# One Conformer mixer of an 11-stage transformer kernel: which channel tile VectorE convolves, in which order, and a norm worked out by halves of the tokens

## The chip, the cores and the metric

The kernel runs on one core of one Trainium2 chip. The metric is the device time of one execution in microseconds (us); lower is better. The core has a matrix engine (TensorE, PE in the rows; its weight loads are PEld), a vector engine (VectorE, DVE), a scalar engine (ScalarE, ACT), GpSimd (POOL) and SyncE (SP). SyncE issues most of the transfers, ScalarE some. Each engine works through its own instructions in order, and semaphores hold an instruction back until what it needs is there.

## The reference

A sequence of 256 tokens by 1024 channels, fp32, passes two attention layers and then four blocks, each a mixer and a squared-ReLU MLP. Block 0 and 3 have a retention mixer, block 2 a short convolution, block 1 the Conformer convolution, which runs once and is all that the change touches, but for one load:

```
def conformer_conv_mixer(x, w_pw1, b_pw1, w_dw, b_dw, ln_g, ln_b, w_pw2, b_pw2):
    h = x @ w_pw1 + b_pw1                      # 256 x 1024 by 1024 x 2048
    a, gate = jnp.split(h, 2, axis=-1)
    h = a * jax.nn.sigmoid(gate)
    h = causal_depthwise_conv(h, w_dw) + b_dw  # 31 taps along the tokens, each channel by itself
    hf = h.astype(F32)
    mean = jnp.mean(hf, axis=-1, keepdims=True)
    var = jnp.mean(jnp.square(hf - mean), axis=-1, keepdims=True)
    hf = (hf - mean) * lax.rsqrt(var + LN_EPS) * ln_g + ln_b
    h = jax.nn.silu(hf)
    return h @ w_pw2 + b_pw2                   # 256 x 1024 by 1024 x 1024
```

## The kernel before

All weights stream through the core once, in chunks of 512 rows by 512 columns (1 MB). Each chunk goes through three buffers: `raw` (loaded by SyncE), `wh` (its high part, a ScalarE cast, `high_to(c)` casts all chunks up to c), and `wl` (the rest, a VectorE subtraction, `low_to(c)`). TensorE multiplies high by high, high by low and low by high, so a product of a chunk takes 48 matmuls. There are three buffers of each kind, so `raw` of chunk c+3 is loaded when `wl` of chunk c is done, and `wh` of c+3 is cast when TensorE has used chunk c. The order of every engine is written out by hand; nothing is scheduled automatically.

The Conformer mixer has chunks +0 to +11 (counted from its first, `first["s", 1]`). Channels lie in 8 tiles of 128 partitions, the 256 tokens along the free dimension.

- Chunks +0 to +3 give gate and value of channel tiles 0 to 3, chunks +4 to +7 those of tiles 4 to 7. ScalarE takes the sigmoids, and `gated(b)` on VectorE makes the gated values `hp` of four tiles, in `HP`.
- Seven tiles are convolved by TensorE, one by VectorE. `four_taps` copies groups of tiles (`a`, `b`, `c` in `TAPS`) between partitions, so that 32 channels at four shifts fill 128 rows; each copy is 16 DMAs. `tap_squares(n)` on VectorE lays out the filter of the n-th tile in `CONV` as small diagonal matrices in `WT` (4 instructions). TensorE then runs 32 pairs of 128x32 by 128x256 fp32 matmuls for the tile, into a bank of PSUM (`whole` when done), and ScalarE copies the result to `HC` (`conv`) and squares it into `SQ` (`sq`).
- Tile 0 is convolved by VectorE: `taps(to)` runs its 31 multiply-adds up to `to`, alternating between two accumulators, and `f0` adds the two.
- The norm goes over channels, which lie across partitions and tiles. VectorE adds the seven first tiles (`sm`) and their squares (`ss`), TensorE sums over partitions by a matrix of ones (`sum`, `squares`), then come mean, variance, square root and reciprocal (`rs`), `centre(j)` and `scale(j)` for pairs of tiles, SiLU and the high part on ScalarE (`ah`), and the low part on VectorE (`low(j)`, `al`).
- Eight matmuls with one row of ones put the bias `b_pw2` into PSUM. Then `rows_out` multiplies by chunks +8 to +11: 96 matmuls, for each half of the columns first all that needs tiles 0 to 3 and then tiles 4 to 7.

## Time and profile before

| what | us |
|---|---|
| median of 3 runs | 2086.62 |
| lowest and highest of the 3 runs | 2083.99, 2089.82 |
| profiled execution, its time | 2083.98 |
| profiled execution, its span | 2082.2 |
| TensorE busy in the span | 2022.8 |
| VectorE, ScalarE busy in the span | 1262.9, 933.9 |

The span runs from the first to the last instruction. In the trace the Conformer's gate and value products stand from 1110 to 1154.2 us, its convolution from there to 1181, the norm to 1190, and the last product to 1214. A row of the timeline has the start, the duration, the engine, the line of the kernel and the operation, output<-input by buffer names and sizes, the number of instructions merged in the row, and in brackets how long the engine sat idle before it and what released it. The name AR stands for one large buffer that holds HC, HP, the tap copies and other tiles; EX, XS and AHL are others.

### The profile page before, as it was taken

The page shows a single profiled execution, that of the slowest core. Times are in us where ns is not written, and L with a number is a line of the kernel's source. Part 1 is how long each engine was busy: PE and PEld are TensorE (multiplying, and loading weights), DVE is VectorE, ACT ScalarE, POOL GpSimd, SP SyncE. Part 2 cuts the span into 40 slices and gives each one's busy share as a digit, 9 for nine tenths or more (in the row PEclk, how much of TensorE's full clock was granted, in tenths as well). Part 3 has the DMA queues.
Part 4 walks back from the last instruction along what each step waited for, and adds up shares of the span by engine and source line. Part 5 has one row for each costly group of instructions (what it writes and reads, how often), then busy time and mean ns, then how long its engine had stood idle before and what let it go on. Part 6 is the DMA issues. An engine that isn't in the chain of part 4 may idle for free.

```text
span 2082.2 us, 29509 instructions
## 1 busy us (share of the span) xinstructions
PE 2022.8 (97%) x12778; PEld 1775.5 (85%) x12778; DVE 1262.9 (61%) x1331; ACT 933.9 (45%) x1051; POOL 65.0 (3%) x89
## 2 busy tenths in 40 slices
PE   7999999999999999999999899999999999999998
PEld 5788898888899898779888689989889979778997
DVE  4775555686645666665556865556664466667544
ACT  6554434654434433444444454444354453335443
POOL 0000000000000000010000000000000000000000
PEclk9999999999999999999999999999999999999999
DMA  7233655433555555445555545546555555444552
GB/s 239 97 107 105 212 193 165 133 133 103 168 193 179 184 187 177 162 160 189 178 200 170 165 141 196 190 142 223 166 178 197 184 180 182 162 162 163 201 182 101
DMA packets 185731, 351.37 MB, mean 169 GB/s; under 512 B 15745, under 2 KB 26881, under 8 KB 185602
## 3 DMA queue, kind: packets, MB, share of 16 engines
q1 hardware_dynamic: 184834, 348.31, 50.0%
q8 instruction: 101, 1.65, 0.3%
q10 hardware_dynamic: 768, 1.17, 0.2%
q14 instruction: 28, 0.23, 0.0%
HBM read 344.31 MB, written 1.05 MB: 166 GB/s over the span
## 4 chain that ended last, share of the span: by engine, by line
PE 89%; DVE 5%; ACT 3%; DMA 2%; issue 1%; ACTq 0%; SPq 0%; POOL 0%; DVEq 0%; POOLq 0%
PE psD L1975 15%; PE psD L1976 15%; PE psD L1980 13%; PE psD L1959 11%; PE psD L1960 11%; PE psD L1964 10%; PE psD L1978 2%; DVE wl L1103 2%; ACT wh L645 1%; PE psD L2255 1%; PE psD L2209 1%; DMA raw<-in_w_in 1%; DVE AHL L1128 1%; DMA raw<-in_w_down 1%; PE psD L2328 1%
## 5 line engine op out<-in xcount | busy, mean ns | idle before, releaser
L1103 DVE TENSOR_TENSOR wl<-raw,wh 128x2048 fp32r<-128x2048 f32 (+2 forms) x328 | 725.9, 2220 | 472.3 <-ACT wh L645 469.9
L645 ACT ACTIVATE wh<-raw 128x2048 fp32r<-128x2048 f32 (+2 forms) x328 | 606.2, 1855 | 539.1 <-PE psD L1978 253.9
L1959 PE MATMUL psD<-AHL,wh 128*128 128x256 f32 x2112 | 599.5, 284 | 5.9 <-DVE wl L1103 3.8
L1960 PE MATMUL psD<-AHL,wh 128*128 128x256 f32 x2112 | 597.4, 283 | 0.0
L1964 PE MATMUL psD<-AHL,wl 128*128 128x256 f32 x1976 | 558.9, 283 | 0.0
L1959 PEld LDWEIGHTS psD<-AHL,wh 128*128 128x128 f32 x2112 | 404.8, 192 | 10.4 <-issue 5.5
L1960 PEld LDWEIGHTS psD<-AHL,wh 128*128 128x128 f32 x2112 | 405.0, 192 | 1.7
L1964 PEld LDWEIGHTS psD<-AHL,wl 128*128 128x128 f32 x1976 | 378.8, 192 | 0.0
L1975 PE MATMUL psD<-wh,HH 128*128 128x512 f32 x880 | 352.2, 400 | 7.2 <-DVE HL L1794 3.2
L1976 PE MATMUL psD<-wl,HH 128*128 128x512 f32 x880 | 349.4, 397 | 0.0
L1980 PE MATMUL psD<-wh,HL 128*128 128x512 f32 x748 | 297.0, 397 | 0.0
L1975 PE MATMUL psD<-wh,AHL 128*128 128x512 f32 (+3 forms) x576 | 225.3, 391 | 19.4 <-DVE wl L1103 14.0
L1976 PE MATMUL psD<-wl,AHL 128*128 128x512 f32 (+3 forms) x576 | 217.2, 377 | 0.0
L1975 PEld LDWEIGHTS psD<-wh,HH 128*128 128x128 f32 x880 | 166.5, 189 | 46.7 <-DVE HL L1794 4.0
L1976 PEld LDWEIGHTS psD<-wl,HH 128*128 128x128 f32 x880 | 166.4, 189 | 37.9 <-issue 0.5
L1980 PE MATMUL psD<-wh,AHL 128*128 128x512 f32 (+3 forms) x483 | 182.2, 377 | 0.0
L1980 PEld LDWEIGHTS psD<-wh,HL 128*128 128x128 f32 x748 | 141.4, 189 | 34.5
L1975 PEld LDWEIGHTS psD<-wh,AHL 128*128 128x128 f32 x576 | 108.9, 189 | 51.4 <-DVE wl L1103 17.8
L1976 PEld LDWEIGHTS psD<-wl,AHL 128*128 128x128 f32 x576 | 109.0, 189 | 18.9 <-issue 1.4
L560 POOL TENSOR_TENSOR ST<-ST,MH 128x1 f32<-128x1 f32 (+1 forms) x58 | 55.3, 957 | 1785.1 <-DVE ST L1156 928.4
L1980 PEld LDWEIGHTS psD<-wh,AHL 128*128 128x128 f32 x483 | 91.2, 189 | 16.6
L940 ACT ACTIVATE VT<-psD 128x1024 f32<-128x1024 f32 x28 | 28.8, 1027 | 96.7 <-PE psD L1962 96.7
(357 smaller groups left out, 1725.4 us busy)
## 6 DMA issues: line engine op xcount, KB each, us to landing
raw<-in_mlp_w SPq DMA_DIRECT2D x128, 1024.0 KB, 5.2
raw<-in_ret_w_in SPq DMA_DIRECT2D x48, 1024.0 KB, 5.1
raw<-in_w_gate SPq DMA_DIRECT2D x20, 1024.0 KB, 5.1
raw<-in_w_up SPq DMA_DIRECT2D x20, 1024.0 KB, 5.1
raw<-in_w_down SPq DMA_DIRECT2D x20, 1024.0 KB, 6.2
raw<-in_w_in SPq DMA_DIRECT2D x16, 1024.0 KB, 7.4
raw<-in_ret_w_out SPq DMA_DIRECT2D x16, 1024.0 KB, 5.1
raw<-in_cf_w_pw SPq DMA_DIRECT2D x12, 1024.0 KB, 5.7
```

The source lines that it names most:

```text
L560: e.tensor_tensor(dst, src, MH[:, 0:n], ALU.pow).then_inc(*up("pool_pow", *event))
L645: e.activation(wh[q % NHL][:, 0:kt * n], raw[q % NRAW][:, 0:kt * n], ACT.Copy).then_inc(*up("act_wh", q))
L940: e.activation(r4, four(2 + b % 2), ACT.Relu).then_inc(*up("act_mlp", "relu", i, b))
L1103: e.tensor_tensor(wl[q % NHL][:, 0:kt * n], raw[q % NRAW][:, 0:kt * n], wh[q % NHL][:, 0:kt * n].bitcast(F32), ALU.subtract).then_inc(*up( ...
L1128: e.tensor_tensor(lo, VT[:, 4 * j:4 * j + 4, ts], hi.bitcast(F32), ALU.subtract).then_inc(*up("dve_norm", "al", i, t, j))
L1959: e.matmul(o, hi[:, k, fs], xh, start=kk == 0 and f % 2 == 0, stop=False, skip_group_check=True)
L1960: e.matmul(o, hi[:, k, fs], xl, start=False, stop=False, skip_group_check=True)
L1964: e.matmul(o, lo[:, k, fs], xh, start=False, stop=kk == 7, skip_group_check=True)
L1975: e.matmul(o[:, 0:n], xh[:, ts], hi[:, k, :], start=begin and k == 0, stop=False)
L1976: e.matmul(o[:, 0:n], xh[:, ts], lo[:, k, :], start=False, stop=False)
L1978: e.matmul(o[:, 0:n], xl[:, ts], hi[:, k, :], start=False, stop=end).then_inc(*up(*event))
L1980: e.matmul(o[:, 0:n], xl[:, ts], hi[:, k, :], start=False, stop=end and k == kt - 1)
```

## The change

The tiles move: TensorE convolves tiles 0 to 6, VectorE tile 7. The copy `a` takes four tiles, `b` two, `c` one. There are more places for `WT`, so that five of the seven filters can be laid out without waiting for a convolution to end, and two more banks (`CBANK`). VectorE lays out three filters ahead of the first gating, between chunk +3 and chunk +4, does eight taps ahead of chunk +9, and adds the norm's sums (`sums(n)`) between its taps; chunk +10's low part comes behind them. The VectorE tile is no more part of these sums: TensorE adds it and its squares by one more matmul each. ScalarE casts chunk +4 ahead of the sigmoids, and SyncE loads chunks +3 and +4 ahead of its wait for the residual (this also in the short-convolution block). Behind the square root, reciprocal, scaling, SiLU, high and low part go by halves of 128 tokens, and the last product takes, for its first half of the columns, all eight tiles of the first 128 tokens and then of the second. The bias matmuls of the second column half wait for the reciprocal of the first token half.

```diff
-CONV = (1, 2, 3, 4, 5, 6, 7)
-TAPS = {"a": (1, 3), "b": (4, 2), "c": (6, 2)}
+CONV = (0, 1, 2, 3, 4, 5, 6)
+TAPS = {"a": (0, 4), "b": (4, 2), "c": (6, 1)}
+CBANK = (0, 1, 2, 3, 6, 7, 0)
...
+        HP, XA, XC, SM, SS, B2W, WT0 = carve(5424, (8, S + 31), (4, 4 * (S + 31)), (4, S + 31), (S,), (S,), (DM,), (1024,))
-        WT = (WT0, XS[:, 0, :], XS[:, 1, :])
+        WT = (AR[:, 2 * DM:2 * DM + 1024], WT0, XS[:, 0, :], XS[:, 1, :], AR[:, 4400:5424], WT0, XS[:, 0, :])
+        WT_BEFORE = {5: 1, 6: 2}
...
                 else:
-                    load_to(first["s", i] + 2)
+                    load_to(first["s", i] + 4)
...
-                    e.wait_ge(*at("dve_cf", "hp", 7))
-                    four_taps(e, "c", (0, 1), "dma_xc0")
+                    e.wait_ge(*at("dve_cf", "hp", 6))
+                    four_taps(e, "c", (0, 1, 2), "dma_xc0")
...
                         first_rows(2 * i + 4, ACT.Identity, True)
                         spread_scale(2 * i + 4)
+                        high_to(c + 2)
                         e.wait_ge(*at("dve_norm", "al", 2 * i + 4, 1, 1))
                         for f in range(4):
...
                 four_taps(e, "b", (2, 3), "dma_xb1")
-                e.wait_ge(*at("dve_cf", "hp", 7))
-                four_taps(e, "c", (2, 3), "dma_xc1")
                 for n, f in enumerate(CONV):
-                    o = bank(n % 4)[:, 0:S]
+                    if n == 2:
+                        e.wait_ge(*at("dve_cf", "hp", 6))
+                        four_taps(e, "c", (3,), "dma_xc1")
+                    o = bank(CBANK[n])[:, 0:S]
                     col = VEC[:, V_BD + f:V_BD + f + 1]
...
-                    if n > 1:
+                    if n > 2:
                         e.wait_ge(*at("dve_cf", "ss", n - 2))
-                    e.activation(SQ[n % 2], o, ACT.Square, bias=col).then_inc(*up("act_cf", "sq", n))
-                    if n == 0:
-                        e.wait_ge(*at("dve_cf", "f0"))
-                        e.activation(SS, HC[:, 0, :], ACT.Square).then_inc(*up("act_cf", "sq0"))
+                    if n == len(CONV) - 1:
+                        e.wait_ge(*at("dve_cf", "f7"))
+                        e.activation(SQ7, HC[:, 7, :], ACT.Square).then_inc(*up("act_cf", "sq7"))
+                    e.activation(SQ[n % 2] if n else SS, o, ACT.Square, bias=col).then_inc(*up("act_cf", "sq", n))
...
-                for j in range(4):
-                    e.wait_ge(*at("dve_cf", "scaled", j))
-                    for f in (2 * j, 2 * j + 1):
-                        e.activation(YS[:, f, :], HC[:, f, :], ACT.Silu, bias=VEC[:, V_LB + f:V_LB + f + 1], scale=VEC[:, V_LG + f:V_LG + f + 1]).then_inc(*up("act_cf", "silu", f))
-                    e.wait_ge(*at("act_cf", "silu", 2 * j + 1))
-                    e.activation(HH[j // 2][:, 2 * (j % 2):2 * (j % 2) + 2, :], YS[:, 2 * j:2 * j + 2, :], ACT.Copy).then_inc(*up("act_cf", "ah", j))
+                for t in range(2):
+                    ts = slice(t * P, (t + 1) * P)
+                    for j in range(4):
+                        e.wait_ge(*at("dve_cf", "scaled", j, t))
+                        for f in (2 * j, 2 * j + 1):
+                            e.activation(YS[:, f, ts], HC[:, f, ts], ACT.Silu, bias=VEC[:, V_LB + f:V_LB + f + 1], scale=VEC[:, V_LG + f:V_LG + f + 1]).then_inc(*up("act_cf", "silu", f, t))
+                        e.wait_ge(*at("act_cf", "silu", 2 * j + 1, t))
+                        e.activation(HH[j // 2][:, 2 * (j % 2):2 * (j % 2) + 2, ts], YS[:, 2 * j:2 * j + 2, ts], ACT.Copy).then_inc(*up("act_cf", "ah", j, t))
...
-                        w = VEC[:, V_DW + k:V_DW + k + 1]
-                        o, x = VR if k % 2 else HC[:, 0, :], HP[:, 0, k:S + k]
+                        w = VEC[:, V_DW + 217 + k:V_DW + 218 + k]
+                        o, x = VR if k % 2 else SQ7, HP[:, 7, k:S + k]
...
+                def sums(n):
+
+                    e.wait_ge(*at("act_cf", "conv", n))
+                    if n > 1:
+                        e.wait_ge(*at("dve_cf", "sm", n - 1))
+                    e.tensor_tensor(SM, SM if n > 1 else HC[:, 0, :], HC[:, n, :], ALU.add).then_inc(*up("dve_cf", "sm", n))
+                    e.wait_ge(*at("act_cf", "sq", n))
+                    if n > 1:
+                        e.wait_ge(*at("dve_cf", "ss", n - 1))
+                    e.tensor_tensor(SS, SS, SQ[n % 2], ALU.add).then_inc(*up("dve_cf", "ss", n))
...
+                def inverse(t):
+                    ts = slice(t * P, (t + 1) * P)
+                    e.wait_ge(*at("act_cf", "sd"))
+                    e.reciprocal(VR[:, ts], VR[:, ts]).then_inc(*up("dve_cf", "rs", t))
...
+                low_to(c + 3)
+                tap_squares(0)
+                tap_squares(1)
+                tap_squares(2)
                 low_to(c + 6)
                 c += 4
                 e.wait_ge(*at("act_norm", "rb", 2 * i + 4))
                 e.wait_ge(*at("pe_used", c - 1))
                 gated(0)
                 low_to(c + 3)
-                tap_squares(0)
-                tap_squares(1)
-                taps(8)
+                tap_squares(3)
+                tap_squares(4)
                 e.wait_ge(*at("pe_used", c + 1))
                 e.tensor_tensor(VT[:, 4:8, :], four(2), bc(RB, 1, 4), ALU.mult).then_inc(*up("dve_cf", "rg", 1))
-                tap_squares(2)
                 low_to(c + 4)
-                taps(12)
                 c += 4
                 e.wait_ge(*at("pe_used", c - 1))
                 gated(1)
+                taps(8)
                 low_to(c + 1)
-                tap_squares(3)
+                tap_squares(5)
                 taps(18)
-                tap_squares(4)
+                sums(1)
+                taps(26)
+                sums(2)
+                sums(3)
                 taps(31)
-                tap_squares(5)
                 e.wait_ge(*at("dve_cf", "tap", 30))
-                e.tensor_tensor(HC[:, 0, :], HC[:, 0, :], VR, ALU.add).then_inc(*up("dve_cf", "f0"))
-                tap_squares(6)
+                e.tensor_tensor(HC[:, 7, :], SQ7, VR, ALU.add).then_inc(*up("dve_cf", "f7"))
+                sums(4)
+                sums(5)
                 low_to(c + 2)
...
                 e.wait_ge(*at("act_cf", "mean"))
                 e.scalar_tensor_tensor(VR, MN, -1.0, MN, ALU.mult, ALU.mult).then_inc(*up("dve_cf", "m2"))
-                centre(0)
                 e.wait_ge(*at("pe_cf", "squares"))
                 e.wait_ge(*at("dve_cf", "m2"))
                 e.scalar_tensor_tensor(VR, bank(5)[:, 0:S], 1.0 / DM, VR, ALU.mult, ALU.add).then_inc(*up("dve_cf", "var0"))
                 e.wait_ge(*at("dve_cf", "var0"))
                 e.tensor_scalar(VR, VR, 0.0, LN_EPS, ALU.max, ALU.add).then_inc(*up("dve_cf", "var"))
+                centre(0)
+                inverse(0)
+                scale(0, 0)
                 centre(1)
-                e.wait_ge(*at("act_cf", "sd"))
-                e.reciprocal(VR, VR).then_inc(*up("dve_cf", "rs"))
-                e.wait_ge(*at("dve_cf", "rs"))
-                scale(0)
-                scale(1)
+                scale(1, 0)
                 centre(2)
-                low(0)
-                scale(2)
+                scale(2, 0)
+                low(0, 0)
                 centre(3)
-                low(1)
-                scale(3)
-                low(2)
-                low(3)
+                scale(3, 0)
+                low(1, 0)
+                inverse(1)
+                low(2, 0)
+                scale(0, 1)
+                low(3, 0)
+                scale(1, 1)
+                scale(2, 1)
+                low(0, 1)
+                scale(3, 1)
+                for j in range(1, 4):
+                    low(j, 1)
                 low_to(c + 4)
...
                 for n, f in enumerate(CONV):
-                    x = "a" if n < 3 else "b" if n < 5 else "c"
+                    x = "a" if n < 4 else "b" if n < 6 else "c"
                     tile, at_ = {"a": XA, "b": XB, "c": XC}[x], (f - TAPS[x][0]) * (S + 31)
                     e.wait_ge(*at("dve_tap", n))
                     if n == 0:
                         e.wait_ge(*at("dma_xa", 3, 3))
-                    elif n in (3, 5):
-                        e.wait_ge(*at(f"dma_x{x}0", 1, 3))
-                        e.wait_ge(*at(f"dma_x{x}1", 3, 3))
-                    if n > 3:
-                        e.wait_ge(*at("act_cf", "sq", n - 4))
+                    elif n == 4:
+                        e.wait_ge(*at("dma_xb0", 1, 3))
+                        e.wait_ge(*at("dma_xb1", 3, 3))
+                        e.wait_ge(*at("dve_cf", "ag", 1))
+                    elif n == 6:
+                        e.wait_ge(*at("dma_xc0", 2, 3))
+                        e.wait_ge(*at("dma_xc1", 3, 3))
+                        e.wait_ge(*at("act_cf", "sq", 0))
...
                 last = len(CONV) - 1
+                e.wait_ge(*at("dve_cf", "f7"))
+                e.matmul(bank(4)[:, 0:S], ONES[:, :], HC[:, 7, :], start=True, stop=False)
                 e.wait_ge(*at("dve_cf", "sm", last - 1))
-                e.matmul(bank(4)[:, 0:S], ONES[:, :], SM, start=True, stop=False)
+                e.matmul(bank(4)[:, 0:S], ONES[:, :], SM, start=False, stop=False)
                 e.wait_ge(*at("act_cf", "conv", last))
                 e.matmul(bank(4)[:, 0:S], ONES[:, :], HC[:, CONV[last], :], start=False, stop=True).then_inc(*up("pe_cf", "sum"))
                 e.wait_ge(*at("dve_cf", "ss", last - 1))
                 e.matmul(bank(5)[:, 0:S], ONES[:, :], SS, start=True, stop=False)
+                e.wait_ge(*at("act_cf", "sq7"))
+                e.matmul(bank(5)[:, 0:S], ONES[:, :], SQ7, start=False, stop=False)
                 e.wait_ge(*at("act_cf", "sq", last))
                 e.matmul(bank(5)[:, 0:S], ONES[:, :], SQ[last % 2], start=False, stop=True).then_inc(*up("pe_cf", "squares"))
...
+                def arrived(j, t):
+                    e.wait_ge(*at("dve_cf", "al", j, t))
+
+                for nb in range(2):
+                    if nb:
+                        e.wait_ge(*at("dve_cf", "rs", 0))
+                    for t in range(2):
+                        e.matmul(psD[nb][:, t, :], ONES[0:1, :], B2[:, nb * 512:(nb + 1) * 512], start=True, stop=False)
                 for nb in range(2):
                     for t in range(2):
-                        e.matmul(psD[nb][:, t, :], ONES[0:1, :], B2[:, nb * 512:(nb + 1) * 512], start=True, stop=False)
-                rows_out(("y", i), c, arrived, True, 2 * i + 5)
+                        for j in range(2):
+                            n = c + 2 * nb + j
+                            if nb == 0:
+                                arrived(2 * j, t)
+                            if t == 0:
+                                e.wait_ge(*at("dve_wl", n))
+                            rows_part(n, psD[nb][:, t, :], t, 4 * j, hid_tile, False, j == 1, ("pe_used", n) if t else ("pe_part", ("y", i), 0, nb) if j else None,
+                                      (lambda: arrived(2 * j + 1, t)) if nb == 0 else (lambda: turned_tokens(2 * i + 5, 0)) if t and j else None)
```

On ScalarE, from the end of the norm ahead of the mixer to the copies of the taps, before (L922 takes the first product, L1001 and L1007 are the sigmoids, wh<-raw is a cast of a chunk, DMA a copy of the taps):

```order
L645 ACTIVATE wh<-raw 128x2048
L922 ACTIVATE AR<-psD,ST 128x512 x2
L707 ACTIVATE EX<-psD 128x256
L1001 ACT_TABLE_LOAD
L1001 ACTIVATE VT<-psD,VEC 128x256 x4
L645 ACTIVATE wh<-raw 128x2048 x4
L1007 ACTIVATE VT<-VT,VEC 128x256 x4
L645 ACTIVATE wh<-raw 128x2048 x3
L342 DMA AHL<-AR 32x571 x8
L342 DMA AR<-AR 32x571 x8
```

and in the change:

```order
L924 ACTIVATE AR<-psD,ST 128x512 x2
L709 ACTIVATE EX<-psD 128x256
L647 ACTIVATE wh<-raw 128x2048
L1004 ACT_TABLE_LOAD
L1004 ACTIVATE VT<-psD,VEC 128x256 x4
L647 ACTIVATE wh<-raw 128x2048 x3
L1010 ACTIVATE VT<-VT,VEC 128x256 x4
L647 ACTIVATE wh<-raw 128x2048 x3
L344 DMA AHL<-AR 32x571 x8
L1026 ACTIVATE AR<-psD,VEC 128x256
```

One cast has moved ahead of the table load and the sigmoids, and the eight copies of group `c` no longer stand ahead of the first result of the convolution.

On VectorE, from the second gating on, in the change (L1821 and L1826 are the gating, L1785 taps, L1109 a chunk's low part, L1766 filters, L1793 and L1797 the sums):

```order
L1821 TENSOR_TENSOR AR<-psD,EX 128x4x256
L1826 SCALAR_TENSOR_TENSOR AR<-AR,VEC,VT 128x256 x4
L1780 TENSOR_SCALAR EX<-AR,VEC 128x256
L1782 TENSOR_SCALAR EX<-AR,VEC 128x256
L1785 SCALAR_TENSOR_TENSOR EX<-AR,VEC,EX 128x256 x6
L1109 TENSOR_TENSOR wl<-raw,wh 128x2048
L1766 TENSOR_TENSOR AR<-KC,AR 128x256 x4
L1766 TENSOR_TENSOR XS<-KC,AR 128x256 x4
L1785 SCALAR_TENSOR_TENSOR EX<-AR,VEC,EX 128x256 x10
L1793 TENSOR_TENSOR AR<-AR 128x256
L1797 TENSOR_TENSOR AR<-AR,EX 128x256
L1785 SCALAR_TENSOR_TENSOR EX<-AR,VEC,EX 128x256 x8
```

Before, 12 taps stood ahead of the second gating and 19 behind it, with four filters (16 instructions) between them and no sums; the change has all 31 taps behind it, with two filters.

On VectorE, behind the last sum, before (L1840 and L1844 to L1846 make the variance, L1784 is `centre`, L1789 `scale`, L1794 `low`):

```order
L1840 SCALAR_TENSOR_TENSOR EX<-AR 128x256
L1784 TENSOR_TENSOR AR<-AR 128x512
L1844 SCALAR_TENSOR_TENSOR EX<-psD,EX 128x256
L1846 TENSOR_SCALAR EX<-EX 128x256
L1784 TENSOR_TENSOR AR<-AR 128x512
L1849 RECIPROCAL EX<-EX 128x256
L1789 TENSOR_TENSOR AR<-AR,EX 128x512 x2
L1784 TENSOR_TENSOR AR<-AR 128x512
L1794 TENSOR_TENSOR HL<-AR,HH 128x512
```

and in the change:

```order
L1109 TENSOR_TENSOR wl<-raw,wh 128x2048
L1862 SCALAR_TENSOR_TENSOR EX<-AR 128x256
L1865 SCALAR_TENSOR_TENSOR EX<-psD,EX 128x256
L1867 TENSOR_SCALAR EX<-EX 128x256
L1801 TENSOR_TENSOR AR<-AR 128x512
L1806 RECIPROCAL EX<-EX 128x128
L1812 TENSOR_TENSOR AR<-AR,EX 128x2x128
L1801 TENSOR_TENSOR AR<-AR 128x512
L1812 TENSOR_TENSOR AR<-AR,EX 128x2x128
L1801 TENSOR_TENSOR AR<-AR 128x512
L1812 TENSOR_TENSOR AR<-AR,EX 128x2x128
L1817 TENSOR_TENSOR HL<-AR,HH 128x2x128
```

The first low part now has one reciprocal and three scalings of half the size ahead of it, three centrings instead of two behind the variance, and a chunk's low part directly ahead of the mean.

## Rows read from the trace of the kernel before

**Rows 1.** The page, part 1: busy time of each engine in the span.

```profile
PE 2022.8 (97%) x12778; PEld 1775.5 (85%) x12778; DVE 1262.9 (61%) x1331; ACT 933.9 (45%) x1051; POOL 65.0 (3%) x89
```

**Rows 2.** Timeline of TensorE, from chunk +4 to the last product's start.

```profile
1131.04 0.36 PE L1959 MATMUL psD<-AHL,wh 128*128 128x256 f32 x1 [1.73 <-DVE wl L1103]
...
1154.23 3.44 PE L2587 MATMUL psD<-AR 128*32 128x256 f32 x59
...
1165.99 3.44 PE L2587 MATMUL psD<-AHL,AR 128*32 128x256 f32 x59 [1.19 <-DMA AHL<-AR]
...
1170.49 3.44 PE L2587 MATMUL psD<-AHL,XS 128*32 128x256 f32 x59 [0.84 <-ACT EX L1025]
...
1173.95 3.44 PE L2587 MATMUL psD<-AR,XS 128*32 128x256 f32 x59
...
1180.69 0.38 PE L2585 MATMUL psD<-AR 128*32 128x256 f32 x1
...
1183.14 3.70 PE L2604 MATMUL psD<-AR,ONES 1*128 1x512 f32 x8
...
1190.04 0.79 PE L1975 MATMUL psD<-wh,HH 128*128 128x512 f32 x1 [3.21 <-DVE HL L1794]
```

**Rows 3.** Timeline of ScalarE and VectorE, ahead of chunk +4.

```profile
1123.50 0.38 ACT L707 ACTIVATE EX<-psD 128x256 f32<-128x256 f32 x1 [1.44 <-PE psD L2030]
...
1126.63 5.53 ACT L645 ACTIVATE wh<-raw 128x2048 fp32r<-128x2048 f32 x3
...
1128.60 6.70 DVE L1103 TENSOR_TENSOR wl<-raw,wh 128x2048 fp32r<-128x2048 f32 x3 [5.37 <-ACT wh L645]
```

**Rows 4.** Timeline of SyncE's and ScalarE's queues: the tap copies, and ScalarE's cast.

```profile
1138.24 11.11 SPq L342 DMA_DIRECT2D AR<-AR  x16
...
1157.52 1.92 ACT L645 ACTIVATE wh<-raw 128x2048 fp32r<-128x2048 f32 x1 [0.80 <-DMA raw<-in_cf_w_pw]
1157.69 6.29 ACTq L342 DMA_DIRECT2D AHL<-AR  x8
```

**Rows 5.** Line 342, the tap copies: ns min/median/max of one issue, first and last start.

```profile
L342 SPq DMA_DIRECT2D AR<-AR x24: 580/592/1571, 1138.2 to 1168.5; - x24
```

**Rows 6.** Timeline of VectorE, during the convolution.

```profile
1155.52 1.22 DVE L1798 TENSOR_TENSOR AR<-psD,EX 128x1024 f32<-128x1024 f32 x1
...
1158.37 2.28 DVE L1103 TENSOR_TENSOR wl<-raw,wh 128x2048 fp32r<-128x2048 f32 x1
1160.57 1.42 DVE L1760 TENSOR_TENSOR AR<-KC,AR 128x256 f32<-128x256 f32 x4
1161.91 0.47 DVE L1779 SCALAR_TENSOR_TENSOR AR<-AR,VEC 128x256 f32<-128x256 f32 x1
...
1164.29 1.42 DVE L1760 TENSOR_TENSOR XS<-KC,AR 128x256 f32<-128x256 f32 x4
...
1176.00 0.41 DVE L1835 TENSOR_TENSOR AR<-AR 128x256 f32<-128x256 f32 x1
```

**Rows 7.** Timeline of VectorE and ScalarE, from the mean to the first low part.

```profile
1182.80 0.43 DVE L1840 SCALAR_TENSOR_TENSOR EX<-AR 128x256 f32<-128x256 f32 x1 [2.70 <-ACT AR L1030]
...
1185.01 1.75 DVE L1849 RECIPROCAL EX<-EX 128x256 f32<-128x256 f32 x1
...
1187.51 1.09 ACT L1036 ACTIVATE AR<-AR,VEC 128x256 f32<-128x256 f32 x2 [1.27 <-DVE AR L1789]
...
1189.30 0.69 DVE L1794 TENSOR_TENSOR HL<-AR,HH 128x512 fp32r<-128x512 f32 x1 [0.62 <-ACT HH L1038]
```

**Rows 8.** Timeline of TensorE in the last product: 13th and 24th matmul.

```profile
1195.24 0.39 PE L1975 MATMUL psD<-wh,HH 128*128 128x512 f32 x1
...
1197.80 0.40 PE L1978 MATMUL psD<-wh,HL 128*128 128x512 f32 x1
```

**Rows 9.** Busy time in windows of 0.5 us; PEclk is the granted clock.

```profile
1188.00:1188.50 0.50, 0.00 (x0) 0.00 (x0) 0.50 (x2) 0.50 (x2) 0.00 (x0) 0.79 0.00 0
...
1195.00:1195.50 0.50, 0.50 (x4) 0.41 (x3) 0.00 (x0) 0.00 (x0) 0.00 (x0) 0.88 0.00 0
```

More of the change, by code:

```diff
@@ L2088, in rows_out @@
                     for t in range(2):
-                        rows_part(c + j, psD[0][:, t, :], t, 4 * j, hid_tile, j == 0 and not seeded, j == 1, ("pe_used", c + j) if t else ("pe_part", s, 0, 0) if j else None,
+                        rows_part(c + j, psD[0][:, t, :], t, 4 * j, hid_tile, j == 0, j == 1, ("pe_used", c + j) if t else ("pe_part", s, 0, 0) if j else None,
                                   None if t else lambda: arrived(2 * j + 1))
@@ L2101, in rows_out @@
                             e.wait_ge(*at("dve_wl", c + 2 + j))
[L2102 removed]
+                        rows_part(c + 2 + j, psD[1][:, t, :], t, 4 * j, hid_tile, j == 0, j == 1, ("pe_used", c + 2 + j) if t else ("pe_part", s, 0, 1) if j else None,
                                   (lambda: turned_tokens(i, 0)) if t and j else None)
```

47 lines of the change are left out of this document (19 added, 28 removed).

## The prediction, made before the changed kernel ran

> **What bounds the kernel now.** I read the busy times of the page first: TensorE is busy for 97% of the span [rows 1], so time can only be won where it waits or runs slow. Then the timeline of TensorE through the one Conformer mixer. The reader is to see four stalls there [rows 2]: 1.73 us ahead of chunk +4, for its low part; 1.19 us ahead of the fourth convolved tile, for the copies of group b; 0.84 us ahead of the fifth, for a square that frees its bank; and 3.21 us ahead of the last product, for the first low part of the normed values. A fifth loss doesn't show as idle time: from 1188.0 to about 1195 the granted clock is down from 2.4 to 1.2 GHz [rows 9], after TensorE's last matmul had ended at 1186.84 (1183.14 + 3.70), and the product starts into it. Its first 12 matmuls take 1195.24 - 1190.04 = 5.20 us; eleven steps at full clock take 1197.80 - 1195.24 = 2.56, or 0.233 each [rows 2, 8]. Twelve would take 2.8, so the low clock costs 2.4 us.
>
> Outside the mixer the change only loads two chunks earlier ahead of the short convolution, and TensorE doesn't wait there for a load. So all must come from 1129 to 1195 us.
>
> **Chunk +4.** Its cast stood behind the sigmoids and began at 1126.63, though ScalarE had been through with the scale at 1123.50 + 0.38 [rows 3]. The three casts take 5.53 us, 1.84 each; a low part takes 2.20 more (1160.57 - 1158.37) [rows 3, 6]. Now the cast begins at 1123.9, ends at 1125.7, and the low part ends at 1128. TensorE had stopped at 1131.04 - 1.73 = 1129.3 [rows 2]. VectorE now lays out three filters ahead of it (1.34 each, 1161.91 - 1160.57 [rows 6]), in 5.37 us in which it was idle [rows 3]: from 1123.2 to 1127.2 even if chunk +3 comes no sooner, so the low part ends between 1128 and 1129.4. The sigmoids, which ended at 1126.6, end 1.84 later, at 1128.5, still ahead of 1129.3, where TensorE wants their bank; without that cover of 0.8 us the rest would be paid. Gain 1.7 (bounds 1.0 and 1.9). The convolution starts at 1152.5 instead of 1154.23.
>
> **The convolution.** From 1154.23 to 1180.69 + 0.38 = 1181.07 it takes 26.84 us; a tile takes 1173.95 - 1170.49 = 3.46 [rows 2], seven of them 24.2, so 2.6 us are waits. The first four tiles now need only group a, which lasts to 1152.5 + 13.8 = 1166.3. Group b's half on ScalarE stands behind chunk +10's cast, which waits for its load until 1157.52; its eight issues take 6.29 us, to 1163.98, and TensorE was released at 1165.99, 2.0 later [rows 2, 4]. At the same hour as before that is 0.3 us before it is wanted. Group c has 12 small copies on SyncE behind eight of b: at 0.69 each (11.11 / 16 [rows 4]) they end by 1169 and land by 1171, wanted at 1173.3. The bank is another one now. Group a is the open one: 16 copies took 11.11 us [rows 4], and with four tiles they carry 4/3 of the bytes. If issuing sets their pace (0.59 us in the median [rows 5]), the last lands at 1138 + 11.1 + 2.0 = 1151.1, 1.4 us early. If bytes do, 14.8 us: TensorE waits until 1154.8, 2.3 us. I take the first, since copies of two tiles, 8 in 6.29 us, are no faster each than those of three. Gain 2.6 (bounds 0 and 2.6); the convolution ends at 1176.7.
>
> **VectorE beside it.** This is what the moved taps could break. From the second gating on it has, by spacing of starts [rows 6]: gating 2.85 (1158.37 - 1155.52), 31 taps at 0.40 (six in 1164.29 - 1161.91 = 2.38) 12.3, two filters 2.7, two low parts 4.4, and 11 additions, 3.7 (0.41 long, and like the taps, 0.47 long and 0.40 apart, they start 0.07 before the one ahead ends). The last filter's place is free when tile 2 is convolved, at 1152.5 + 10.4 = 1162.9; VectorE is there at 1162.1 and waits 0.8. Together 26.7 us from 1152.6: it is through at 1179.3. So the mean's first use starts 2.6 us behind the convolution's end, where it was 1182.80 - 1181.07 = 1.7 [rows 2, 7]. TensorE's extra matmul for tile 7 (0.4 us) is hidden under this; without that cover it would cost that.
>
> **The norm.** From there to the product it was 1190.04 - 1182.80 = 7.2 us [rows 2, 7]. `centre(0)` leaves the variance's chain: 0.5 less. The reciprocal of half the tokens has no row: its lower bound is the 0.41 of a 256-wide addition [rows 6], its upper one the 1.75 of the whole [rows 7]; it is the same operation, so nearer to half, 0.9: 0.85 less. One half-size `scale` instead of a whole one ahead of SiLU: 0.3 less. Then VectorE has two centrings (0.6) and two half scalings (0.34) ahead of the first low part, 2.1 us with their waits where 1189.30 - 1187.51 = 1.8 was [rows 7]: 0.3 more. Half a low part: 0.35 less. That makes 5.5, and the product starts at 1184.8, 5.2 us sooner than 1190.04. (Bounds of this stretch: 4.8 and 6.5.) Each later pair of tiles for the first tokens follows in 1.3 us, and six matmuls take 1.4, so TensorE should not stop again. Chunk +11's cast now waits for 36 instead of 24 matmuls of the 96; its cast and low part need 1.84 + 2.20 + some 0.3, and it is wanted 24 matmuls, 5.6 us, later: hidden by 1.2 us.
>
> The row of a 256-wide addition says 0.41 us, that of a 512-wide low part 0.69 [rows 6, 7]: half the width is more than half the time, and that speaks against halves. I have taken the four half-size operations ahead of the first low part at 0.34 apart.
> The Trainium skill (VectorE: DVE Perf Modes, the section on the TRN2 errata) says that each instruction pays a fixed cost, gives (N + 151)/0.96 ns for fp32 additions, 424 ns for 256 elements, and advises tiles of 512 and more. By that and with nothing overlapped, the sum below would be 0.3 us smaller; the durations of the trace agree with it, the spacing of the starts is shorter.
>
> **The clock.** TensorE's idle time ahead of the product shrinks to below 1 us, since half of the bias matmuls now wait for the reciprocal. Whether the clock then stays, no row of before says: there it fell 1.2 to 1.5 us after the last of them had ended [rows 2, 9]. Bounds: nothing won, or 2.4. I take half, 1.2.
>
> **Sum.** 1.7 + 2.6 + 0.9 (the end of convolution to the product, 9.0 then and 8.1 now) = 5.2, and 1.2: 6.4 us. The profiled execution took 2083.98 us (span 2082.2 and 1.8 around it): 2077.6. It lay 2.6 us below the median of three, so for the median 2086.62 - 6.4 = 2080.2.
>
> **The rivals.**
> 1. *The stalls go as computed, and the clock holds too.* 5.2 + 2.4 = 7.6 us, 2079.0. For it: the long idle stretch is gone. Against: the bias matmuls are all that stands in most of that time, and before it fell soon behind them.
> 2. *The stalls go, the clock falls all the same.* The stretch without full matmuls is still from 1179.6 to 1184.8. 5.2 us or less, 2081.5. This (0.25) and rival 1 (0.35) are the two ends of my forecast, 0.6 together.
> 3. *The copies or VectorE take the place of the stalls.* Group a by its bytes: 2.3 us of waiting, the last filter and all of VectorE's chain as late, and group b's loads behind it. Gain 2.5 to 3, 2084. For it: group a has just 1.4 us to spare. VectorE has none: what it loses, the product loses. Chance 0.25.
> 4. *Slower.* The first convolution waits for group a by far more. The longest single issue of such a copy was 1.57 us [rows 5]; if the wider rows made all 16 like it, they would take 25 us and land at 1165, 12.6 us late: 2086.6 - 6.4 + 12.6 = 2092.8. It decides from 7.8 us more than the 11.1, 1.18 us a copy. Against it: two and three tiles cost the same. Chance 0.06.
> 5. *The change does nothing*, since what it removes was covered: speaks against it that each stall has its row. The 0.09 left are for this and for what I have not seen.
>
> **How the numbers follow.** A measurement of this kernel tells about 0.3% (6.3 us) from no change. My forecast lies on that line. Faster: 0.30 of rival 1's 0.35, 0.13 of rival 2's 0.25 (three runs scatter by more than what it lacks), 0.03 of the rest, 0.46. Slower: rival 4's 0.06 and 0.02 of the unseen, 0.08. Within 0.3%: what is left, 0.46. The range goes from 2075.0 (7.9 us, and 3 us for what three runs differ by, 2083.99 to 2089.82) to 2086.5, which takes in rival 3; what is left out is rival 4 and part of 5.
>
> **What would show it.** In the changed kernel's trace: no idle time ahead of chunk +4; a convolution of 24.2 us without a gap; VectorE's low part of chunk +10 ending 2 to 3 us behind it; the product's first matmul 8.1 us behind it, and no wait in it; and the clock at 1195 us and before. Wrong it would be by a wait of TensorE for group a, by a gap on VectorE between taps and sums, or by the first low part coming later than SiLU's.

## The result and the profile after

| | before | after |
|---|---|---|
| median of 8 runs, us | 2085.47 | 2079.20 |
| lowest and highest | 2083.99, 2089.82 | 2078.48, 2082.63 |
| profiled execution, its time and span | 2083.98, 2082.2 | 2079.72, 2077.9 |

The ratio of the times is 0.9972, 95% interval [0.9962, 0.9982]: 5.8 us less, between 3.8 and 7.9. That is clear of no change, and just short of the 0.3% (6.3 us) that the prediction took for what a measurement of this kernel tells.

Two traces are best compared from a mark to a mark, since the clock also falls elsewhere, and not in the same places. The first mark is the last matmul of the MLP ahead of the mixer that waits for a low part, the second the first of the MLP behind it that waits for a chunk. TensorE's timeline of the kernel before has them at

```profile
1110.64 0.50 PE L1975 MATMUL psD<-wh,AHL 128*128 128x512 f32 x1 [0.35 <-DVE AHL L1128]
...
1219.94 0.50 PE L1975 MATMUL psD<-wh,AHL 128*128 128x512 f32 x1 [0.66 <-DVE wl L1103]
```

and that of the changed kernel, with the rows between that answer to [rows 2, 8]:

```profile
1111.41 0.50 PE L2003 MATMUL psD<-wh,AHL 128*128 128x512 f32 x1 [0.35 <-DVE AHL L1134]
...
1129.09 0.28 PE L1987 MATMUL psD<-AHL,wh 128*128 128x256 f32 x1
...
1152.94 3.44 PE L2618 MATMUL psD<-AR 128*32 128x256 f32 x59
...
1167.17 3.44 PE L2618 MATMUL psD<-AHL,AR 128*32 128x256 f32 x59 [0.20 <-DVE EX L1785]
...
1177.37 0.38 PE L2616 MATMUL psD<-AR,XS 128*32 128x256 f32 x1
...
1180.46 1.98 PE L2641 MATMUL psD<-AR,ONES 1*128 1x512 f32 x4
1182.92 3.72 PE L2641 MATMUL psD<-AR,ONES 1*128 1x512 f32 x4 [0.48 <-DVE EX L1806]
1186.57 0.80 PE L2003 MATMUL psD<-wh,HH 128*128 128x512 f32 x1
...
1190.95 0.40 PE L2003 MATMUL psD<-wh,HH 128*128 128x512 f32 x1
...
1215.66 0.50 PE L2003 MATMUL psD<-wh,AHL 128*128 128x512 f32 x1 [0.65 <-DVE wl L1109]
```

From mark to mark it is 109.30 us before and 104.25 after: 5.05 us won. The stall ahead of chunk +4 is gone, and of those in the convolution one small gap is left. The product's first matmul has no bracket: TensorE didn't idle ahead of it, but was still in the second four bias matmuls, which take 3.72 us where the first four take 1.98. The clock says why. Stretches of the changed kernel, the granted clock third from the right:

```profile
1180.00:1183.00 3.00, 2.52 (x8) 0.87 (x6) 2.75 (x7) 2.50 (x3) 0.00 (x0) 1.00 0.45 120
1183.00:1186.00 3.00, 3.00 (x4) 1.03 (x4) 2.93 (x7) 2.66 (x8) 0.00 (x0) 0.50 0.59 229
1186.00:1188.00 2.00, 2.00 (x4) 1.16 (x4) 1.97 (x4) 1.94 (x6) 0.00 (x0) 0.50 0.00 0
1188.00:1190.00 2.00, 2.00 (x6) 1.57 (x5) 1.73 (x6) 1.63 (x5) 0.00 (x0) 0.54 0.00 0
```

It is down from 1183 to about 1189.8, 5 us sooner than in [rows 9]: 3.6 us ahead of the product's first matmul, where in the kernel before it fell 1.8 us ahead of it. The stages, in us, for this and for the kernels of the experiments, one trace each (start of the convolution from the first mark; its length; from its start to the first use of the mean on VectorE, and to the product; the product's first twelve matmuls; mark to mark):

| kernel | start | length | to the mean's use | to the product | first 12 | marks |
|---|---|---|---|---|---|---|
| before | 43.59 | 26.84 | 28.57 | 35.81 | 5.20 | 109.30 |
| after | 41.53 | 24.81 | 27.18 | 33.63 | 4.38 | 104.25 |
| e1_cast_only | 41.53 | 28.37 | 30.10 | 37.34 | 4.36 | 107.94 |
| e2_whole_tail | 41.51 | 24.39 | 27.18 | 34.42 | 5.28 | 106.18 |
| e3_bias_now | 41.52 | 24.39 | 27.17 | 32.96 | 4.40 | 103.59 |
| e4_bias_rows | 41.56 | 24.87 | 27.18 | 32.95 | 2.90 | 102.12 |
| e5_low_part_late | 41.53 | 24.78 | 26.72 | 32.86 | 2.90 | 102.01 |
| e6_sum_on_vector | 41.52 | 24.96 | 27.86 | 33.64 | 2.90 | 102.77 |
| e7_both | 41.53 | 25.04 | 27.04 | 32.84 | 2.89 | 101.97 |
| e8_cast_late | 45.08 | 24.38 | 27.18 | 33.66 | 4.35 | 107.81 |
| e9_rows_now | 41.51 | 24.39 | 27.18 | 32.97 | 4.33 | 103.52 |
| e10_before_rows | 45.98 | 26.88 | 28.60 | 35.85 | 4.34 | 110.88 |

VectorE and ScalarE of the changed kernel, from the end of the sums to the first low part, answer to [rows 6, 7]:

```profile
1177.92 2.28 DVE L1109 TENSOR_TENSOR wl<-raw,wh 128x2048 fp32r<-128x2048 f32 x1
...
1179.27 0.38 ACT L1034 ACTIVATE AR<-psD 128x256 f32<-128x256 f32 x1 [0.32 <-PE psD L2625]
...
1180.12 0.42 DVE L1862 SCALAR_TENSOR_TENSOR EX<-AR 128x256 f32<-128x256 f32 x1
...
1181.92 0.95 DVE L1806 RECIPROCAL EX<-EX 128x128 f32<-128x128 f32 x1
...
1183.43 0.88 ACT L1042 ACTIVATE AR<-AR,VEC 128x128 f32<-128x128 f32 x2 [0.28 <-DVE AR L1812]
...
1185.44 0.42 DVE L1817 TENSOR_TENSOR HL<-AR,HH 128x256 fp32r<-128x256 f32 x1
```

The mean's use has no bracket: VectorE comes to it straight from chunk +10's low part, when the mean (ScalarE's row) has been ready for 0.47 us. The queues, which answer to [rows 4]:

```profile
1138.61 10.48 SPq L344 DMA_DIRECT2D AR<-AR  x16
...
1160.88 9.85 SPq L344 DMA_DIRECT2D AR<-AR  x12
...
1159.03 1.92 ACT L647 ACTIVATE wh<-raw 128x2048 fp32r<-128x2048 f32 x1 [2.23 <-DMA raw<-in_cf_w_pw]
1159.09 6.30 ACTq L344 DMA_DIRECT2D AHL<-AR  x8
```

### The profile page after: what moved, and what is told of

Read it like the earlier page. It is cut to its first block, busy times and chain, and to the rows that moved or that the text cites. A ratio compares the mean times of both kernels' runs of the same rounds, so it can differ in the third digit from the quotient of the medians.

```text
span 2077.9 us, 29537 instructions
## 1 busy us (share of the span) xinstructions
PE 2025.8 (97%) x12782; PEld 1778.0 (86%) x12782; DVE 1263.8 (61%) x1338; ACT 937.2 (45%) x1063; POOL 65.2 (3%) x89
## 4 chain that ended last, share of the span: by engine, by line
PE 90%; DVE 5%; ACT 2%; DMA 1%; issue 1%; SPq 0%; POOL 0%; DVEq 0%; POOLq 0%; ACTq 0%
PE psD L2003 15%; PE psD L2004 15%; PE psD L2008 13%; PE psD L1987 11%; PE psD L1988 11%; PE psD L1992 11%; PE psD L2006 2%; DVE wl L1109 2%; ACT wh L647 1%; PE psD L2283 1%; DMA raw<-in_w_in 1%; PE psD L2237 1%; DVE AHL L1134 1%; PE psD L2356 1%; PE psD L2357 1%
## 5 line engine op out<-in xcount | busy, mean ns | idle before, releaser
L1109 DVE TENSOR_TENSOR wl<-raw,wh 128x2048 fp32r<-128x2048 f32 (+2 forms) x328 | 726.1, 2220 | 463.6 <-ACT wh L647 461.0
```

The source lines that it names most:

```text
L1109: e.tensor_tensor(wl[q % NHL][:, 0:kt * n], raw[q % NRAW][:, 0:kt * n], wh[q % NHL][:, 0:kt * n].bitcast(F32), ALU.subtract).then_inc(*up( ...
```

## The experiments

**The early cast alone.** On the kernel before:

```diff
-                    load_to(first["s", i] + 2)
+                    load_to(first["s", i] + 4)
...
                         spread_scale(2 * i + 4)
+                        high_to(c + 2)
```

> The kernel before, with chunk +4's cast ahead of the sigmoids and its load two chunks earlier; nothing else of the change. Theory 1 (mine: the parts of the change need each other): the idle 1.73 us ahead of chunk +4 goes and the convolution starts about 1.7 us sooner, but group b of the shifted copies lands at its own hour (ScalarE's half of it stands behind chunk +10's cast, which waits for its load until about 1157.5), so the wait ahead of the fourth convolved tile grows from 1.2 to about 2.9 us. The product starts at most 0.5 us sooner and the time stays within 0.5 us of the kernel before. Theory 2 (the gains add up): the product starts 1.7 us sooner and the kernel takes 1.7 us less.

Median 2084.44 us (11 runs) against 2085.26, ratio 0.9994 [0.9985, 1.0003]. TensorE's timeline in its convolution:

```profile
1150.70 3.44 PE L2588 MATMUL psD<-AR 128*32 128x256 f32 x59
...
1163.16 3.44 PE L2588 MATMUL psD<-AHL,AR 128*32 128x256 f32 x59 [1.89 <-DMA AHL<-AR]
...
1167.74 3.44 PE L2588 MATMUL psD<-AHL,XS 128*32 128x256 f32 x59 [0.91 <-ACT EX L1026]
...
1171.95 3.44 PE L2588 MATMUL psD<-AR,XS 128*32 128x256 f32 x59 [0.55 <-DMA AR<-AR]
```

The convolution starts 2.06 us sooner and lasts 1.53 longer: TensorE waits 1.89 us for the copies of group b where it waited 1.19 [rows 2], and 0.55 us for those of group c, for which it didn't wait before. The wait for group b grew less than theory 1 said (to 2.9), but with group c's the outcome is that of theory 1: the product starts 0.53 us sooner, and alone this part is worth little. The other 0.83 us between the marks is the low clock. It lasts 6.8 us in both traces, but in this one it fell 3.6 us ahead of the product and in the kernel before 1.8 us, though the bias matmuls start 2.07 us behind the convolution's end in both. The code of the tail is the same in both, so twelve matmuls in 4.36 instead of 5.20 us don't need the changed tail.

**The cast back behind the sigmoids**, on the changed kernel:

```diff
-                        high_to(c + 2)
```

> The changed kernel with chunk +4's cast back behind the sigmoids; the earlier load, tiles, taps, sums and halves stay. Theory 1 (with the new tiles the chain of VectorE hangs on the second gating, which waits for TensorE to be through with chunk +7): the stall ahead of chunk +4 is back and all behind it is later by its 2.1 us, to the product; 2.1 us slower than the changed kernel. Theory 2 (the cover that was found for the copies takes it up: group b and group c are late by their own hour): the convolution loses its remaining gap of 0.4 us and the kernel is at most 1.5 us slower.

Median 2081.78 (10 runs), ratio 0.9983 [0.9974, 0.9992], 2.3 us more than the ratio of the changed kernel gives. The convolution loses its gap of 0.4 us, as theory 2 had it (24.38 instead of 24.81), but from its start to the mean's use it is 27.18 us as in the change, and to the product 33.66 instead of 33.63: what the start loses, the product loses, which is theory 1. This execution lost 3.56 us between the marks. Its first matmul of chunk +4, and two stretches of it:

```profile
1130.37 0.45 PE L1986 MATMUL psD<-AHL,wh 128*128 128x256 f32 x1 [1.83 <-DVE wl L1108]
```

```profile
1129.00:1131.00 2.00, 0.63 (x3) 0.66 (x4) 2.00 (x2) 2.00 (x2) 0.00 (x0) 0.87 0.00 0
1131.00:1134.00 3.00, 3.00 (x17) 3.00 (x16) 3.00 (x2) 0.49 (x1) 0.00 (x0) 0.52 0.83 279
```

The clock fell as the stall ended, and 17 matmuls start in 3 us where 27 do in the same stretch of the changed kernel. The kernel before had a stall of 1.73 us there [rows 2] and its clock stayed up. So the stall cost 2.06 us in the trace of before, and in this one 1.5 more. One trace each doesn't show how often the clock falls there.

**The tail of before.** The changed kernel with one reciprocal, whole scalings, SiLU and low parts, the bias matmuls all at once, and the old order of the product (the diff of that part, taken back).

> The changed kernel with the tail of the kernel before: whole tokens behind the norm (one reciprocal of 256, whole scalings, SiLU and low parts), all eight bias matmuls at once, TensorE's order as before; taps, tiles, sums and the early cast as in the change. Theory 1: the product starts 9.6 us behind the convolution's end (2.4 to the mean's use and 7.2 from there, as before) where the change has 8.8, and its first twelve matmuls all run at the low clock, 5.2 us where the change has 4.4: 1.6 us slower than the changed kernel, about 4.5 us faster than before. Theory 2 (halves pay a fixed cost twice and bring nothing): as fast as the changed kernel or faster.

Median 2081.42 (11 runs), ratio 0.9982 [0.9973, 0.9991]; between the marks 1.93 us more than the change. The product starts 0.79 us later and its twelve matmuls take 0.90 longer (the rest is what the two traces differ by behind them). The 0.79 bear out theory 1 and rule out theory 2. The 0.90 are what theory 1 said, but e1, with the same tail, took 4.36 us for its twelve, so that they belong to the tail is not shown. By the medians the tail of before costs 2.1 us, and the two intervals overlap. The halves themselves bring more than 0.79: from the mean's use to the product it is 7.24 here and 5.8 in e3_bias_now, where no bias matmul stands in the way, 1.4 us.

**The bias matmuls.** Two edits. One takes the wait away:

```diff
-                    if nb:
-                        e.wait_ge(*at("dve_cf", "rs", 0))
```

The other lets them use all rows of the array:

```diff
-        ET, GA, B2 = (ET0, ET1), (GA0, GA1), B2W[0:1, :]
+        ET, GA, B2 = (ET0, ET1), (GA0, GA1), B2W
...
-                    e.dma_start(B2[:, :], A["row"][0:1, R_B2:R_B2 + DM]).then_inc(*landed("dma_b2"))
+                    e.dma_start(B2[:, :], A["row"][0:1, R_B2:R_B2 + DM].to_broadcast([P, DM])).then_inc(*landed("dma_b2"))
...
-                        e.matmul(psD[nb][:, t, :], ONES[0:1, :], B2[:, nb * 512:(nb + 1) * 512], start=True, stop=False)
+                        e.matmul(psD[nb][:, t, :], ID, B2[:, nb * 512:(nb + 1) * 512], start=True, stop=False)
```

> The changed kernel, in which the second four bias matmuls no longer wait for the first reciprocal. Theory 1 (the low clock reaches the bias matmuls in the change, and these, not the first low part, set the product's start): they are through before the clock falls at about 1183, the product starts with the first low part at 1186.0 instead of 1186.6, 8.2 us behind the convolution. The clock falls all the same, so the time stays within 1 us of the changed kernel. Theory 2 (that wait keeps TensorE busy and so shortens the low clock): the low clock reaches further into the product, the first twelve matmuls take 5.2 us or more instead of 4.4, and the kernel is 0.5 to 1.5 us slower.

> The changed kernel, in which the eight bias matmuls use all 128 rows of the array instead of one: the bias row is loaded into all 128 partitions and multiplied by the identity, in as many columns as before. Theory 1 (the clock falls because these matmuls, alone for 4 to 6 us, work on one row only): the granted clock stays at full through the bias matmuls, the second four take 1.9 instead of 3.7 us, the product starts with the first low part at 1186.0, and its first twelve matmuls take 2.8 to 3.5 instead of 4.4 us: 1.5 to 2.2 us faster than the changed kernel. Theory 2 (the clock follows idle time alone, or the columns): nothing moves, the clock falls at 1183 and the first twelve take 4.4 us.

> The kernel of e4_bias_rows (bias matmuls on all 128 rows), in which the second four no longer wait for the first reciprocal, as in e3_bias_now. TensorE then stands idle for about 3 us ahead of the product. Theory 1 (it is the work on one row that brings the clock down, and that wait is not needed): the clock holds, the product starts 8.1 us behind the convolution's end and its first twelve matmuls take 2.9 us; as fast as e4_bias_rows. Theory 2 (the wait spreads the bias matmuls over the stretch, and without it 3 us of idle time bring the clock down): the first twelve take 4 to 5.2 us, 1 to 2.3 us slower than e4_bias_rows.

> The kernel before, with only its eight bias matmuls on all 128 rows. The product starts when it did, 9.0 us behind the convolution's end, after 3.2 us of idle time. Theory 1 (one row alone brings the clock down): the clock holds, the first twelve matmuls take 2.9 instead of 5.2 us, 2.3 us faster than before. Theory 2 (the change's waits, not the rows, make the difference, or 3.2 us of idle time are enough): the clock falls as before and nothing is won.

| | with the wait | without it |
|---|---|---|
| one row | after: 0.9972 [0.9962, 0.9982] | e3: 0.9969 [0.9959, 0.9979] |
| 128 rows | e4: 0.9957 [0.9942, 0.9972] | e9: 0.9962 [0.9949, 0.9975] |

The traces tell more than the times. TensorE's timeline of e4_bias_rows, with both sets of four at full clock, and its stretches:

```profile
1182.02 1.88 PE L2641 MATMUL psD<-AR,KC 128*128 128x512 f32 x4
1184.50 1.98 PE L2641 MATMUL psD<-AR,KC 128*128 128x512 f32 x4 [0.60 <-DVE EX L1806]
1187.48 0.50 PE L2003 MATMUL psD<-wh,HH 128*128 128x512 f32 x1 [1.00 <-DVE HL L1817]
...
1190.38 0.40 PE L2003 MATMUL psD<-wh,HH 128*128 128x512 f32 x1
```

```profile
1183.00:1186.00 3.00, 2.40 (x7) 0.75 (x5) 2.86 (x6) 2.66 (x5) 0.00 (x0) 1.00 0.97 312
1186.00:1188.00 2.00, 1.00 (x4) 0.48 (x3) 1.97 (x5) 1.97 (x6) 0.00 (x0) 1.00 0.11 41
```

The clock doesn't fall, the product waits for the low part as it was meant to, and twelve matmuls take 2.90 us. The same in the traces of e5, e6 and e7, which are built on it: four of four. With one row it fell in all six (before, after, e1, e2, e3, e8). In e3_bias_now and e9_rows_now the eight bias matmuls stand in one block behind the sums. Their rows, the first matmul of the product, and the stretches, first of e3:

```profile
1180.36 4.90 PE L2639 MATMUL psD<-AR,ONES 1*128 1x512 f32 x8
1186.19 0.79 PE L2003 MATMUL psD<-wh,HH 128*128 128x512 f32 x1 [0.93 <-DVE HL L1817]
...
1180.00:1183.00 3.00, 3.00 (x8) 1.28 (x8) 2.85 (x6) 2.12 (x3) 0.00 (x0) 0.95 0.41 91
1183.00:1186.00 3.00, 2.26 (x3) 0.33 (x1) 2.83 (x7) 2.66 (x7) 0.00 (x0) 0.50 0.67 259
```

and of e9:

```profile
1179.78 3.60 PE L2639 MATMUL psD<-AR,KC 128*128 128x512 f32 x8
1185.71 0.80 PE L2003 MATMUL psD<-wh,HH 128*128 128x512 f32 x1 [2.33 <-DVE HL L1817]
...
1180.00:1183.00 3.00, 3.00 (x8) 1.14 (x6) 2.75 (x7) 2.07 (x3) 0.00 (x0) 1.00 0.59 164
1183.00:1186.00 3.00, 0.67 (x2) 0.29 (x2) 2.93 (x7) 2.70 (x7) 0.00 (x0) 0.91 0.48 186
```

This pair separates the rows from idle time. In e3 TensorE has no pause from the convolution on, and yet the clock falls at 1182.7, among the bias matmuls, which then take 4.90 us. In e9 the same block on 128 rows runs through at full clock in 3.60 us, and the clock falls only at 1185.5, after 2.1 us of idle time. It also stays down for less: 3.4 us in e9 and in e10, against 6.8 us in before, after, e1, e3 and e8, and 10.2 in e2.

In e3 the product starts 0.67 us sooner than in the changed kernel, at the low part: so in the change the slow bias matmuls, not the norm, set the product's start, as theory 1 had it (only that they are through before the clock falls did not come true), and the wait that the change gave them brings nothing while they are on one row. In e9 128 rows alone don't hold the clock either: 2.33 us of idle time, and it is down (4.33 us for twelve). My theory 1 of e9 fell; in these traces the clock held only with both, all rows and the wait that spreads them. The times don't tell e9 from e4; between the marks it is 1.40 us more.

e10_before_rows came to 2085.25 (11 runs) against 2083.95, ratio 1.0006 [0.9998, 1.0015]. The clock fell within the 3.40 us of idle time, as theory 2 had it, and the twelve matmuls took 4.34 us, which e1 reached with one row as well. And something came that neither expected: ScalarE's cast of a gate chunk, ahead of the mixer,

```profile
1123.36 1.91 ACT L645 ACTIVATE wh<-raw 128x2048 fp32r<-128x2048 f32 x1 [6.92 <-DMA raw<-in_cf_w_pw]
```

waits for its load, which stands on SyncE's queue behind the bias load that is now 512 KB. The convolution starts 2.39 us later. In e4 the same bias load costs nothing (its convolution starts at 41.56, as in the change), and there two more chunks are loaded ahead of it: the `+ 4` of the change is the cover. That the bias load is what held the chunk up is read from the order of the queue; no run shows it alone.

**What bounds the stretch to the norm.** On e4_bias_rows, either or both of two edits:

```diff
                 sums(5)
-                low_to(c + 2)
```

```diff
                 sums(5)
...
+                e.tensor_tensor(SM, SM, HC[:, 7, :], ALU.add).then_inc(*up("dve_cf", "sm", 7))
...
+                e.tensor_tensor(SS, SS, SQ7, ALU.add).then_inc(*up("dve_cf", "ss", 7))
...
-                e.matmul(bank(4)[:, 0:S], ONES[:, :], HC[:, 7, :], start=True, stop=False)
...
-                e.matmul(bank(5)[:, 0:S], ONES[:, :], SQ7, start=False, stop=False)
```

The second also has ScalarE take the square of tile 7 ahead of the last convolved tile.

> The kernel of e4_bias_rows, with the low part of chunk +10 (2.2 us of VectorE ahead of the norm) moved behind the norm's last low part, beside that of chunk +11. Theory 1 (behind the convolution TensorE's six sums come nearly as late as VectorE): the mean's first use starts 0.4 us sooner, but the variance still waits for the sum of the squares, so the product starts at most 0.1 us sooner. Theory 2 (VectorE alone sets the product's start): 0.4 us sooner. For both: the slot that this low part frees is that of chunk +13's load, which then starts some 13 us later; if TensorE comes to wait for chunk +13, the kernel loses several us behind the mixer.

> The kernel of e4_bias_rows, with tile 7 added to the two sums by VectorE (two additions ahead of the low part of chunk +10) instead of two more matmuls into the sums on TensorE, and the square of tile 7 taken before the last convolved tile is read. Theory 1 (VectorE bounds the stretch to the norm): VectorE is 0.7 us longer, the mean's use starts 3.0 instead of 2.3 us behind the convolution's end, and the product 0.6 to 0.7 us later. Theory 2 (the sums on TensorE bound it): two sums fewer there, the squares 0.9 us sooner, and the product starts no later than now.

> The edits of e5_low_part_late and of e6_sum_on_vector together, on the kernel of e4_bias_rows. Theory 1 (each of the two alone leaves the other one as the bound): the squares are summed 0.5 us sooner and VectorE is free by then, the product starts 7.6 instead of 8.1 us behind the convolution's end. Theory 2 (something else, such as the table load of the square root, bounds it): no more than e5_low_part_late brings. The late load of chunk +13 as there.

e5: median 2075.63 (4 runs), ratio 0.9951 [0.9937, 0.9964]. The mean's use comes 0.46 us sooner, the product 0.09: theory 1. VectorE's timeline shows where the rest stays, the variance waiting for the sum of squares:

```profile
1176.37 0.42 DVE L1861 SCALAR_TENSOR_TENSOR EX<-AR 128x256 f32<-128x256 f32 x1 [1.66 <-ACT AR L1034]
1177.25 0.42 DVE L1864 SCALAR_TENSOR_TENSOR EX<-psD,EX 128x256 f32<-128x256 f32 x1 [0.46 <-PE psD L2630]
```

No wait for chunk +13 came of the late load.

e6: one run, 2076.71. VectorE is 0.68 us longer and the product 0.69 later, theory 1: giving one sum to TensorE is worth that.

e7: median 2075.62 (5 runs), ratio 0.9953 [0.9939, 0.9966]. The product starts 0.11 us sooner than in e4, not 0.5: theory 1 fell. TensorE's row of the one gap in its convolution, and its first sum,

```profile
1166.00 3.44 PE L2622 MATMUL psD<-AHL,AR 128*32 128x256 f32 x59 [0.45 <-DMA AHL<-AR]
...
1176.98 0.70 PE L2625 MATMUL psD<-AR,ONES 128*128 128x256 f32 x2 [0.41 <-DVE AR L1861]
```

which waits 0.41 us for the addition that was put on VectorE. Ahead of the norm the chains are within half a microsecond of each other: in the changed kernel the mean is ready 0.47 us before VectorE uses it, and the last sum of squares ends 0.12 us before VectorE reads it, so 2.2 us less on VectorE can bring only 0.1.

e4, e5 and e7 come to 0.9951 to 0.9957, some 9 to 10 us under before. By the ratios that is 3 to 4 us under the change, but their intervals overlap its own; the marks say 2.1 to 2.3. Between the three the times can't tell.

## Why the prediction was right, and where its sizes were off

The time was forecast at 2080.2 and is 2079.2, by the mechanism that was forecast. But part of that nearness is luck: the terms came to 6.4 us where the marks show 5.05, and the median of three from which the forecast subtracted lay 1.15 us above that of eight; the two errors are opposite.

- *Chunk +4, 1.7 (1.0 to 1.9).* Measured 2.06, outside the bounds. They were taken from the idle time of the row, 1.73, which begins when the last matmul's modelled duration of 0.28 ends. Matmuls here start 0.12 apart, so a stall costs 0.16 more than its bracket, and the first matmuls behind it start wider apart. The order of events was right: cast at 1124.54, low part at 1126.48, sigmoids over by 1129.3, with some 0.5 us left of the 0.8 that was said to cover them.
- *The convolution, 2.6 (0 to 2.6).* It takes 24.81 instead of 26.84: 2.03. Issuing paced group a, 10.48 us for four tiles against 11.11 for three, so rival 3 by bytes is out. The gap that is left is group b, which by the forecast would be there "0.3 us before it is wanted". From the first mark chunk +10's cast began at 47.62 us instead of 46.88, and the eight issues behind it with it. The gap's row names a tap of VectorE, for which this tile doesn't wait; e7's row of the same gap, shown above, names the copies, and it is there in the five traces in which ScalarE's last issue of group b ends 12.4 us or more behind the convolution's start (after, e4 to e7), and not in the four where it ends by 12.0 (e2, e3, e8, e9).
- *VectorE beside it.* From the convolution's start to the mean's use 26.8 was forecast, 27.18 measured; 2.37 behind the end, where 2.6 was said. That it has nothing to spare is shown: 27.17 or 27.18 in six kernels, whether the convolution takes 24.4 or 24.9 us. So the gap of group b costs nothing, and the 0.42 us between the two would not have been won.
- *The norm, 5.5 (4.8 to 6.5).* To the end of the first low part it is 5.74. Every term has the right sign and came out 0.04 to 0.12 smaller than forecast: 0.40 for `centre(0)` (0.5), 0.73 for the half reciprocal (0.85), 0.26 for the half scaling (0.3), 0.22 lost between SiLU and the low part (0.3), 0.27 for the half low part (0.35). But the product itself starts 6.45 behind the mean's use. **This is the step that failed**: it let the product start with the low part and had the clock reach only the product. The low clock came 5 us sooner and took the bias matmuls, 0.7 us on the path.
- *The clock, 1.2 (0 to 2.4).* The twelve matmuls took 0.82 us less than in the trace of before. That the change earned it is not shown, as e1 had the same with the tail of before. The 1.2 was a guess half way between its bounds. That "half of the bias matmuls now wait for the reciprocal" was argued as something that shortens the idle time and so might hold the clock; after and e3 show that on one row it doesn't, and e4 that on 128 rows it does.

In the sum: 2.06 + 2.03 + 0.15 (8.97 to 8.82 behind the convolution's end, where 0.9 was forecast) + 0.82 = 5.06. From the convolution's start to the product 32.3 was forecast and 33.63 measured: 0.4 of the difference in VectorE's chain, 0.2 in the norm, 0.7 in the bias matmuls. The profiled executions differ by 4.3 us only, as the changed one lost 0.77 ahead of the first mark. Rival 2 (the clock falls all the same, at most 5.2 us) is what happened; rival 1 became true in e4 (7.2 us between the marks, where it said 7.6). Of rival 3 there is group b's small gap, on nobody's path; nothing of rival 4. The range's lower end is 0.7 us lower than its own terms give (2086.6 - 7.9 - 3 = 2075.7); nothing hangs on it.

By the formula of the Trainium skill (VectorE: DVE Perf Modes, the TRN2 errata) 256 elements take an estimated 424 ns, and 0.41 to 0.43 us is what the halves' scalings and low parts show. Its advice, tiles of 512 elements and more, speaks against the halves. Here they pay, 7.24 us with whole tokens (e2) against 5.79 (e3), since only the first half stands on the path.

## What to carry to other kernels

Look at what TensorE does in a stretch in which it waits: filling it with matmuls that use one row of the array did not keep the clock here; the same number with all rows did, once they were spread so that no pause was longer than 1.5 us. When two engines are level (VectorE and the copies here), a part of a change that gains 2 us gives back 1.5 unless the others come with it, so cost the parts together, and test them alone. Compare traces between two marks around the change, don't take a stall at the length of its bracket, and don't credit a change with where the clock happens to fall in one trace.
